# Two pairs of token tiles at the block junctions of an fp32 transformer kernel

## The reference

```python
# first block
h = rms_norm(x, norm_mix)
proj = h @ w_in                      # stick-breaking attention and gated linear attention
mix = sigmoid(gate_sb) * (o_sb @ w_proj_sb) + sigmoid(gate_gla) * (o_gla @ w_proj_gla)
x = x + mix @ w_out                                  # -> junction h_mlp0
h2 = rms_norm(x, norm_mlp)
x = x + square(relu(h2 @ w_ff1)) @ w_ff2             # w_ff1 1024x4096, w_ff2 4096x1024
x = rms_norm(x, norm_final)                          # -> junction h_mix1
# layer i = 0 (differential attention), i = 1 (short convolution)
h = rmsnorm(x, norm_mixer_pre[i])
m = diff_attention(h, ...) or short_conv(h, ...)
x = x + rmsnorm(m, norm_mixer_post[i])               # -> junctions h_mlp1, h_mlp2
h = rmsnorm(x, norm_mlp_pre[i])
x = x + rmsnorm(square(relu(h @ mlp_w_up[i])) @ mlp_w_down[i], norm_mlp_post[i])
                                                     # -> junctions h_conv, out
```

## Time and profile before

| | us |
|---|---|
| median of 3 runs | 2171.01 (2169.66 to 2172.40) |
| time of the profiled execution | 2170.88 |
| its span, first to last instruction | 2169.1 |
| TensorE busy | 2033.6 (94%) |
| VectorE busy | 1044.3 (48%) |
| ScalarE busy | 749.1 (35%) |
| GpSimd busy | 161.8 (7%) |
| mean granted TensorE clock | 0.970 of full speed |

### The profile page before, as it was taken

How to read it: one execution, slowest core, us unless ns; L and a number is a source line. 1 busy time by engine, 2 the same in 40 slices (tenths; PEclk the granted TensorE clock), 3 DMA queues, 4 the chain that set the end, 5 groups by cost and what they waited for, 6 DMA issues and landing times.

```text
span 2169.1 us, 23378 instructions
## 1 busy us (share of the span) xinstructions
PE 2033.6 (94%) x9821; PEld 1704.0 (79%) x9821; DVE 1044.3 (48%) x957; ACT 749.1 (35%) x866; POOL 161.8 (7%) x327
## 2 busy tenths in 40 slices
PE   6998989999999999989998699999979987999997
PEld 5777768878788888878887588888868766888886
DVE  3346467764542433356775643333452555333434
ACT  3353462424331322345454432232241224231322
POOL 1000033000100000031000300000030012000001
PEclk9999999999999999989999799999989988999999
DMA  4311212222323223222222222322212232222221
GB/s 172 97 57 41 78 39 78 78 78 78 106 99 97 97 97 97 97 73 86 83 64 78 64 96 96 97 96 95 97 60 97 82 111 68 97 97 97 97 97 58
DMA packets 97997, 188.28 MB, mean 87 GB/s; under 512 B 3982, under 2 KB 16288, under 8 KB 97920
## 3 DMA queue, kind: packets, MB, share of 16 engines
q1 hardware_dynamic: 93888, 176.17, 24.7%
q0 software_dynamic: 3744, 10.21, 1.6%
q10 hardware_dynamic: 288, 0.79, 0.1%
HBM read 184.01 MB, written 2.10 MB: 86 GB/s over the span
## 4 chain that ended last, share of the span: by engine, by line
PE 81%; DVE 8%; ACT 4%; POOL 3%; issue 3%; DMA 1%; SPq 0%; POOLq 0%; ACTq 0%; DVEq 0%
PE ps L689 51%; PE ps L813 8%; PE ps L701 5%; PE ps L714 3%; PE ps L1031 2%; PE ps L1037 2%; PE ps L917 1%; POOL small L535 1%; PE ps L739 1%; PE ps L1056 1%; ACT arena L1533 1%; PE ps L1181 1%; ACT w_hi L1230 1%; ACT qk L1295 1%; POOL small L537 1%
## 5 line engine op out<-in xcount | busy, mean ns | idle before, releaser
L1673 DVE TENSOR_TENSOR w_lo<-w_raw,w_hi 128x2048 fp32r<-128x2048 f32 x126 | 288.7, 2292 | 764.6 <-ACT w_hi L1230 764.6
L1230 ACT ACTIVATE w_hi<-w_raw 128x2048 fp32r<-128x2048 f32 x126 | 241.3, 1916 | 874.4 <-PE ps L689 758.4
L689 PE MATMUL ps<-a_hi,w_hi 128*128 128x512 f32 x992 | 386.0, 389 | 0.0
L689 PE MATMUL ps<-a_lo,w_hi 128*128 128x512 f32 x992 | 386.0, 389 | 0.0
L689 PE MATMUL ps<-a_hi,w_lo 128*128 128x512 f32 x992 | 385.9, 389 | 0.0
L689 PE MATMUL ps<-w_hi,h_hi 128*128 128x512 f32 x672 | 263.6, 392 | 11.2 <-DVE h_lo L1717 7.7
L689 PE MATMUL ps<-w_lo,h_hi 128*128 128x512 f32 x672 | 263.1, 391 | 0.0
L689 PE MATMUL ps<-w_hi,h_lo 128*128 128x512 f32 x672 | 262.9, 391 | 0.0
L689 PEld LDWEIGHTS ps<-a_hi,w_hi 128*128 128x128 f32 x992 | 186.3, 188 | 38.6
L689 PEld LDWEIGHTS ps<-a_hi,w_lo 128*128 128x128 f32 x992 | 186.2, 188 | 38.5
L689 PEld LDWEIGHTS ps<-a_lo,w_hi 128*128 128x128 f32 x992 | 186.3, 188 | 38.4
(11 more groups left out here) (342 smaller groups left out, 3290.4 us busy)
## 6 DMA issues: line engine op xcount, KB each, us to landing
w_raw<-in_w_ff SPq DMA_DIRECT2D x32, 1024.0 KB, 5.3
w_raw<-in_mlp_w_up SPq DMA_DIRECT2D x32, 1024.0 KB, 5.6
w_raw<-in_mlp_w_down SPq DMA_DIRECT2D x32, 1024.0 KB, 5.1
w_raw<-in_w_in SPq DMA_DIRECT2D x26, 1024.0 KB, 5.0
w_raw<-in_attn_w_qkv SPq DMA_DIRECT2D x12, 1024.0 KB, 5.1
w_raw<-in_conv_w_in SPq DMA_DIRECT2D x12, 1024.0 KB, 5.2
w_raw<-in_w_proj_gla SPq DMA_DIRECT2D x4, 1024.0 KB, 5.1
w_raw<-in_w_out SPq DMA_DIRECT2D x4, 1024.0 KB, 5.0
```

The source lines that it names most:

```text
L689: last = mm(ps[:, bank0 + j], left, right, start=(k == 0 and x == 0), stop=(k == QUAD * quads - 1 and x == 2), skip_group_check=halves)
L1230: nc.scalar.activation(w_hi[:, s], w_raw[:, s], ACT.Copy).then_inc(hi_ready, 1)
L1673: tt(w_lo[:, s], w_raw[:, s], w_hi[:, s].bitcast(F32), ALU.subtract).then_inc(lo_ready, 1)
```

## The change

Every junction but the first (`h`) is done in two pairs of tiles. The last block ahead of a junction (`w_out`, the last block of each MLP, `conv_out`) is computed in the order (tile 0, quad 0), (1, 0), (0, 1), (1, 1), (2, 0), (3, 0), (2, 1), (3, 1). The norm steps of VectorE, ScalarE and GpSimd are written pair by pair, with the split of the next product's quad 0 (`mid_split`) inside the first pair and that of quad 1 (`last_split`) inside the second. TensorE transposes tiles 0 and 1, multiplies both quads on tokens 0 to 255, transposes tiles 2 and 3, and multiplies both quads on tokens 256 to 511. At `h_mix1` the same is done with the q and k loads; k goes to banks 2 and 3. `w_o` keeps its order. On TensorE the last round of each MLP is unrolled too, so the loop runs over rounds 1 and 2. The junction `h` and `proj_gla` keep their order in other words. The diff, cut to its core:

```diff
@@ stat_count
-            first = 4 * add
             if turn_ is None:
-                return first + i + 1
-            if n == add:
-                return first + (1 if i == 0 else 2 * i)
-            return first + (2 * i + 3 if i < TT - 1 else 2 * TT)
+                return 4 * add + i + 1
+            return 4 * add + 4 * (i // 2) + 2 * (n - add) + i % 2 + 1
@@ gpsimd, refine_tiles
-                for s_ in range(TT + 1):
-                    if add is not None and s_ < TT:
-                        refine(name, add, s_)
-                    if turn_ is not None and s_ > 0:
-                        refine(name, turn_, s_ - 1)
+                for pair in ((0, 1), (2, 3)):
+                    for n in (add, turn_):
+                        for i in pair:
+                            if n is not None:
+                                refine(name, n, i)
@@ tensor, last block (for ordered products, and block 3 of an MLP's last round)
+            def ordered_block(p, blk, u, hi, lo):
...
+                pe.wait_ge(banks_free, p.b + blk - 1)
+                pe.wait_ge(lo_ready, n + 1)
...
+                tile(0, 0)
+                tile(1, 0)
+                pe.wait_ge(lo_ready, n + 2)
+                tile(0, 1).then_inc(tile_done, 1)
+                tile(1, 1).then_inc(tile_done, 1)
+                tile(2, 0)
+                tile(3, 0).then_inc(quad_done, 1)
+                tile(2, 1).then_inc(tile_done, 1)
+                tile(3, 1).then_inc(quad_done, 1)
@@ tensor, entry of the next product (instead of turn_tiles)
+            def begin(name, p):
+                bank0 = 4 * (p.b % 2)
+                pe.wait_ge(banks_free, after_block[name] - 1)
+                turn_tile(name, 0)
+                turn_tile(name, 1)
+                pe.wait_ge(turned_lo, turn_base[name] + 4)
+                for qi in range(2):
+                    pe.wait_ge(lo_ready, p.q + qi + 1)
+                    multiply_half(a_hi, a_lo, slot_of(p, 0, qi), bank0, 0, qi=qi)
+                turn_tile(name, 2)
+                turn_tile(name, 3)
+                pe.wait_ge(turned_lo, turn_base[name] + 8)
+                for qi in range(2):
+                    multiply_half(a_hi, a_lo, slot_of(p, 0, qi), bank0, 1, qi=qi).then_inc(quad_done, 1)
@@ tensor, mlp
                 rounds(0)
-                with pe.Fori(1, ROUNDS) as r:
+                with pe.Fori(1, ROUNDS - 1) as r:
                     rounds(r)
+                rounds(ROUNDS - 1)
@@ tensor, h_mix1 (instead of turn_tiles and one pair in halves)
+            for z_ in range(2):
+                pe.wait_ge(lo_ready, first_pair + z_ + 1)
+                pair_half(a_hi, a_lo, (first_pair + z_) % 2, 2 * z_, 0, range(KT))
...
+            for z_ in range(2):
+                wh, wl = pair_w[(first_pair + z_) % 2]
+                for f in range(2):
...
-            paired = [4]
+            paired = [8]
@@ scalar, junction
+                moved(0)
+                moved(1)
+                if both:
+                    added(0)
+                mid_split()
+                if both:
+                    added(1)
+                if turn_ is not None:
+                    high(name, 0)
+                    high(name, 1)
+                moved(2)
                 last_split()
+                moved(3)
+                if both:
+                    added(2)
+                    added(3)
+                if turn_ is not None:
+                    high(name, 2)
+                    high(name, 3)
@@ vector, junction
+                moved(0)
+                moved(1)
+                dve.wait_ge(grow_in, 16 * rows)
+                added(0)
+                added(1)
...
+                scaled(name, turn_, 0)
+                mid_split()
+                scaled(name, turn_, 1)
+                moved(2)
+                moved(3)
+                low(name, 0)
+                low(name, 1)
+                added(2)
                 last_split()
+                added(3)
+                scaled(name, turn_, 2)
+                scaled(name, turn_, 3)
+                low(name, 2)
+                low(name, 3)
@@ scalar and vector, the held splits
-            phase_to_junction("w_out")
-            junction("h_mlp0", held_split("w_out"))
+            body(ph["w_out"], 0, 0)
+            junction("h_mlp0", held_split("w_out", 0), held_split("w_out", 1))
...
-            junction("h_mlp1", held_split("w_o"))
+            junction("h_mlp1", lambda: None, held_split("w_o", 0))
```

More of the change, by code:

```diff
@@ L1270, in rounds @@
                         blk = r * 4 + u
-                        for qi in range(1 if tail and u == 3 else 2):
+                        for qi in range(0 if tail and u == 3 else 2):
                             split(p, blk, u, qi)
@@ L1298, in square, with high @@
                 nc.scalar.activation(y, lv, ACT.Exp, scale=-0.5).then_inc(guess_ready, 1)
-            def junction(name, last_split, early_split=None):
-                tile0, kind, add, adds, turn_, _ = junctions[name]
+            def high(name, i):
+                for half in range(2):
+                    act.wait_ge(turned, turn_base[name] + 2 * i + half + 1)
+                    nc.scalar.activation(a_hi[:, 4 * half:4 * half + 4, P * i:P * (i + 1)],
+                                         ps[:, tile_bank(name, i, half)].rearrange("p (a b) -> p a b", a=4),
+                                         ACT.Copy).then_inc(turned_hi, 1)
@@ L1323, in junction, with moved, added @@
-                last_split()
+                        act.wait_ge(x_in[s_], 16)
+                        square("h", 0, s_, x_tm)
+                    if s_ == 3:
+                        first_split(0)
+                    if s_ >= 3:
+                        high("h", s_ - 3)
+                first_split(1)
+            def junction(name, mid_split, last_split):
+                tile0, kind, add, adds, turn_, _ = junctions[name]
+                def moved(i):
+                    if i < TT - 1:
+                        act.wait_ge(tile_out, tile0 + i + 1)
+                    else:
+                        act.wait_ge(banks_free, after_block[name])
+                    square(name, turn_ if add is None else add, i, y_tm if kind == "P" else x_tm)
+                def added(i):
+                    act.wait_ge(resid_ready, 4 * adds + i + 1)
+                    square(name, turn_, i, x_tm)
+                both = turn_ is not None and add is not None
+                moved(0)
[9 more added lines that the diff above has]
+                moved(2)
+                last_split()
+                moved(3)
[5 more added lines that the diff above has]
+                    high(name, 3)
@@ L1356, in _ @@
             act.wait_ge(eps_set, 1)
-            junction("h", lambda: first_split(1), lambda: first_split(0))
+            begin_h()
             def sbq_round(blk, bank0):
@@ new lines, in scaled, with low @@
+            def scaled(name, n, i):
+                dve.wait_ge(rstd_ready, stat_count(name, n, i))
+                stt(y_tm[:, i], x_tm[:, i], rstd[n % 2][:, i:i + 1], g_turn, ALU.mult, ALU.mult).then_inc(normed, 1)
+            def low(name, i):
+                for half in range(2):
+                    dve.wait_ge(turned_hi, turn_base[name] + 2 * i + half + 1)
+                    cs = (slice(None), slice(4 * half, 4 * half + 4), slice(P * i, P * (i + 1)))
+                    tt(a_lo[cs], ps[:, tile_bank(name, i, half)].rearrange("p (a b) -> p a b", a=4),
+                       a_hi[cs].bitcast(F32), ALU.subtract).then_inc(turned_lo, 1)
@@ L2290, in _ @@
             body(ph["w_o"], 0, 0, add_tokens(y_tm))
-            junction("h_mlp1", add_tile("w_o", y_tm), 5, held_split("w_o"))
+            junction("h_mlp1", add_tile("w_o", y_tm), 5, lambda: None, held_split("w_o", 0))
             clear_y(dve, 1)
             mlp("mlp1", 4 + 16, 16, y_tm, 3 * 6)
-            junction("h_conv", add_tile("mlp1", y_tm), 7, held_split("mlp1"))
+            junction("h_conv", add_tile("mlp1", y_tm), 7, held_split("mlp1", 0), held_split("mlp1", 1))
             def conv(k):
```

256 lines of the change are left out of this document (123 added, 133 removed).

## The result

The changed kernel takes 2154.67 us, the median of 4 runs (2154.09 to 2157.36). The kernel before took 2171.7 (4 runs, 2169.66 to 2172.91) beside it. The ratio is 0.9929, with a 95% interval of 0.9917 to 0.9942: 17.0 us faster by the medians and 15.4 by the ratio (12.6 to 18.0 by its interval), where 20.5 were forecast. The time lies inside the forecast's own range (2145 to 2156), 4.2 us above the predicted value.

A forecast was written before the change was run, and what follows sets the result against it. TensorE and its waits bound the kernel (81% of the chain that ended last). Terms -7.6 - 8.2 + 0.4 - 1.0 - 2.6 - 1.5 = -20.5 us give 2150.5 us, own range 2145 to 2156, 8 in 10: 2140 to 2160.

The forecast's parts named there:

- Starts of the first halves: At five junctions, first 256-token products were to start 4.1, 5.1, 17.7, 6.6, 6.6 us after the last block's matmuls.
- GpSimd held by the splits: Each weight split on VectorE holds GpSimd's refinement between the norms until it ends; bounds 0 and 2.29 us per split.
- rival B: First gap lowers the clock only at h_mlp1, and splits don't hold GpSimd: -13.8 us, 2136.7 us; chance 0.17.
- First clock fall: TensorE's wait before the first halves lowers its clock once per junction, charged 2.0 us.
- Second wait: Between transposes of tile 3 and second halves, TensorE waits for a_lo: 1.8 us at five junctions, no clock fall charged.
- rival A: The second wait also lowers the clock at five junctions, 2.0 us each: 10 us, 2160.5 us; chance 0.20.
- h_mix1: At q and k loads, window 33.7 us against 39.4, scores start at 48.5; gain 1.0, bounds 0 and 2.5.
- signs of being wrong: h_conv's first halves start before 4 or after 9, TensorE waits for weights, or windows hold but stages behind are longer.
- h_mlp1, out: At h_mlp1, window 46.9 us, gaining 2.6; at the kernel's end, last addition ends at 7.1, gaining 1.5.
- Last block, unrolling, weights of quad 1: Reordering the last block costs 0 us; unrolled MLP round 0, bounds -1 and +2; quad 1's weights arrive in time.
- rival C: Split of quad 1's weights, behind addition 2 on VectorE, comes late and TensorE waits in first halves: +7, 2178; chance 0.04.
- Rival D: ScalarE's or GpSimd's order puts tile 1 some 4 us later at four junctions: +16 us, 2166.5; chance 0.07.

The follow-up runs named there:

- e2_fill: Changed kernel with the transposes of tiles 2 and 3 placed ahead of the last 24 and 12 matmuls of the first halves: 2143.1 us, ratio 0.9882.
- e1_kfirst: Changed kernel where, after h_mix1, k's second bank is copied before q's rounding and k rotated before the next q load's weight split: 2151.17 us, ratio 0.9919.
- e8_best: Changed kernel with transposes moved as in e2_fill, tile 2's move ahead of scaling 1, and k first with the next split behind k's low part: 2139.42 us.
- e10_best_again: Same kernel as e8_best, timed again: 2139.93 us, ratio 0.9862.
- e9_best_idle: e8_best plus idle matmuls in gaps ahead of the first halves (12 and 10 at h_conv and h_mlp2, 10 at h_mix1): 2138.42 us, ratio 0.986.
- e3_late: Changed kernel with the old order in the last block (quad 0 for all tiles, then quad 1 tile by tile): 2180.07 us, ratio 1.0048.
- e4_unroll: Kernel before the change with only the last round of each MLP unrolled on TensorE: 2172.11 us, ratio 1.0005.
- e7_warm: Changed kernel with 14 idle matmuls of 256 columns in each of two gaps ahead of the first halves, at h_conv and h_mlp2: 2151.66 us, ratio 0.9912.

## Why the prediction was right, point by point

- **Starts of the first halves.** Forecast 4.1, 5.1, 17.7, 6.6, 6.6 us after E; measured 3.9, 5.2, 17.6, 6.5, 6.5. Every one is within 0.2, so the order of the norms' steps is as it was worked out.
- **GpSimd held by the splits.** Right. The row of GpSimd under quad 0's split at h_conv, with the split and the scaling behind it, answers to the earlier trace rows:

```profile
1575.01 2.29 DVE L1747 TENSOR_TENSOR w_lo<-w_raw,w_hi 128x2048 fp32r<-128x2048 f32 x1
1575.23 2.12 POOL L534 TENSOR_TENSOR small<-small 128x1 f32<-128x1 f32 x1
1578.20 1.28 DVE L1852 SCALAR_TENSOR_TENSOR y_tm<-x_tm,small,qk 128x1024 f32<-128x1024 f32 x1 [0.91 <-POOL small L537]
```

  An instruction of 0.2 us lasts 2.12, until the split ends, and the split keeps its own 2.29. The Trainium skill, SBUF — State Buffer, "Who interferes with whom", has this contention for a VectorE instruction with two SBUF inputs and a GpSimd instruction that reads SBUF; the trace agrees. Half of rival B rested on the opposite and fell.
- **First clock fall, 2.0 per junction.** Right in size at h_conv and h_mlp2 (first halves 13.95 and 13.8 against 11.6), 2.7 at h_mlp1, 1.4 at h_mix1, none at h_mlp0, where the gap was 2.0 us, in the profiled execution or in any of the eight others with the new order of the last block. The rows that the 2.0 came from add up to 2.4 (0.8 in the transposes, 1.6 in the matmuls). That h_mlp0 is 1.7 better than forecast is this missing fall: this part of rival B came true there. It is luck for the sum, in which it offsets about half of the second wait's clock.
- **Second wait.** Its length was right (1.9 against 1.8), its clock wrong: I charged none, and it fell in 13 of 20 cases at 1.5 us. That is the mis-sized term of the sum, 3 us in the profiled execution and up to 7.5. It is rival A at three quarters of its price and at two junctions of three. e2_fill shows it by taking the wait away. The term for the stretch from tile 2's transposes to the second halves was too small as well: 3.35 us in the sum, 3.8 in this profile at each junction.
- **h_mix1.** The steps to the scores held (48.5). The window did too (33.6 against 33.7). I took 1.0 net of bounds 0 to 2.5; measured was a loss of 1.4 over the whole stretch in this execution. This is one of the signs of being wrong that the prediction names: the window holds and the stage behind it is longer, by 3.8 us. The charge for the low clock behind the 3.3 us of idle was too small (1.5 taken, about 3 in this execution), and nothing was charged for a fall further on. Behind 3.1 to 3.6 us of idle ahead of the scores the clock fell in six profiles of six, for 3.4 to 10.2 us; behind 1.6 or less (e1_kfirst, e8_best, e10_best_again, e9_best_idle) in none of four.
- **h_mlp1, out.** 47.4 against 46.9; the last addition ends 7.1 after E, as forecast.
- **Last block, unrolling, weights of quad 1.** The last block takes no longer in the new order, and without that order the change loses (e3_late); unrolling costs 0 (e4_unroll). TensorE never waits for quad 1's weights in the changed kernel, so rival C did not happen; the 0.37 in e9_best_idle shows that the slack is small once the clock holds. Rival D fell with the first point.

The sum: -20.5 forecast, -13.5 in the profiled spans, -17 in the medians. Of the 7.0 between the sum and the spans, the second halves' clock is 3.0 and first halves and second wait that were each 0.3 to 0.5 longer than taken are 1.5 (h_conv and h_mlp2 together), the stretch behind h_mix1 2.4, h_mlp1 0.5, the fall ahead of the first junction 1.1; h_mlp0 gives back 1.6. The terms add up to 6.9. The difference between spans and medians is that the profiled execution was the slowest of its kernel, 2.7 above its median, and the one before 0.8 under its own. So the steps held and the sum was 3.5 to 6 us too good, less than the terms that were too small, because one charged fall did not come.

## What to carry to other kernels

When a product is cut so that it can begin on half of its rows, the cut makes a second wait between transposes and first use. Fill it with work of the first half: here moving two groups of transposes 24 and 12 matmuls forward was worth 10 to 12 us, two thirds of what the whole change had given. And look for what stands behind a moved instruction in its engine's order: pairing alone lost 10 us, and at each of four junctions the start was late by the length of the weight split that stood between two steps of the norm. Compare two profiles stage by stage only when the clock fell at the same places in both.

## What the runs showed of the hardware that was not expected

- The same program in two executions has the clock fall after the same 1.9 us wait in 2 of 5 places and then in 5 of 5; over all profiles with that wait it is 19 of 28. With 0.15 us of waiting in its place it fell in none of 20. In these profiles the fall came three times behind a wait ahead of tile 2's transposes instead (1.85, 2.19 and 2.51 us), and once not (2.50).
- The length of the wait doesn't settle it. At h_mlp0, 1.9 to 2.0 us of idle behind 16 transposes brought no fall ahead of the first halves in nine profiles of nine; ahead of the second halves of the same junction, 1.9 us behind 16 transposes did in four of six. No run shows what makes the difference.
- The granted clock does not rise at once when work comes back: at h_conv 25 matmuls of 256 columns start at the distance of the 1.2 GHz level, over 5.3 us.
- Keeping TensorE busy with idle matmuls does keep the clock at 1.00 in the first halves (11.6 us against 13.95, e7_warm), but when the work it waits for is nearly as late, it turns into a wait: 2.3 us saved, 1.1 kept.
